# A two-block kernel on one core: the first wait of a preparation stands two pieces later, weight loads stand ahead of stores, and the last layer norm works on tokens

## What is computed

```python
def layer_norm(t, g, b):
    mu = jnp.mean(t32, axis=-1, keepdims=True)
    var = jnp.mean(jnp.square(t32 - mu), axis=-1, keepdims=True)
    y = (t32 - mu) * lax.rsqrt(var + NORM_EPS)
    return y * g + b
...
u, gate, q_mem = _split(h @ lru_w_in[j], [TOK_WIDTH, MIX_WIDTH, MEM_WIDTH])
tok = rg_lru_branch(u, ...)
y = jnp.concatenate([tok, mem_out], axis=-1) * jax.nn.silu(gate)
h = layer_norm(ALPHA * h + y @ w_out[layer], ln_g[layer], ln_b[layer])
```

## Time and profile before

| what | us |
|---|---|
| median of 3 runs | 3521.47 |
| lowest, highest | 3514.03, 3525.67 |
| the profiled execution | 3513.61 |
| its span | 3511.8 |
| PE busy in it | 3248.4 |
| DVE busy in it | 1852.3 |

### The profile page before, as it was taken

One profiled execution on the slowest core, in us unless ns is written; L12 is line 12 of the kernel. 1 busy time (PEld: TensorE's weight loads), 2 busy tenths in 40 slices (PEclk: granted clock), 3 DMA queues, 4 the chain that ended last, 5 costly groups with the idle time before them and its releaser, 6 DMA issues. The chain is left out here.

```text
span 3511.8 us, 46419 instructions
## 1 busy us (share of the span) xinstructions
PE 3248.4 (92%) x18084; PEld 2592.9 (74%) x18084; DVE 1852.3 (53%) x2662; ACT 1158.3 (33%) x2270; POOL 1555.9 (44%) x1195
## 2 busy tenths in 40 slices
PE   6898999999799999889999999999897999999796
PEld 4766787788598988668888888888775666777465
DVE  4288844546445455586633363336312666565736
ACT  5244431333333333331211021102223665145723
POOL 1215635455143341266666666665451001654432
PEclk9988879999899999999999999999997999999898
DMA  4345435232343342353333333334434221222112
GB/s 179 102 141 150 145 116 181 92 92 70 96 128 106 98 131 63 113 152 93 94 98 99 98 93 99 96 96 114 130 105 124 76 61 43 88 83 60 48 54 78
DMA packets 521310, 358.60 MB, mean 102 GB/s; under 512 B 92561, under 2 KB 477446, under 8 KB 520070
## 3 DMA queue, kind: packets, MB, share of 16 engines
q1 hardware_dynamic: 510438, 325.22, 32.0%
q0 software_dynamic: 4608, 16.78, 1.6%
q10 hardware_dynamic: 6048, 13.63, 1.1%
HBM read 276.85 MB, written 78.18 MB: 101 GB/s over the span
## 5 line engine op out<-in xcount | busy, mean ns | idle before, releaser
L2409 PE MATMUL psum<-place,place 128*128 128x512 f32 x2126 | 856.4, 403 | 63.2 <-POOL place L2387 29.3
L2410 PE MATMUL psum<-place,place 128*128 128x512 f32 x2126 | 837.8, 394 | 0.0
L2411 PE MATMUL psum<-place,place 128*128 128x512 f32 x2126 | 836.9, 394 | 0.0
L2385 POOL CAST place<-place 128x1024 fp32r<-128x1024 f32 (+3 forms) x302 | 298.3, 988 | 1097.0 <-PE psum L2411 650.1
L2387 POOL TENSOR_TENSOR place<-place,place 128x1024 fp32r<-128x1024 f32 (+3 forms) x302 | 692.1, 2292 | 24.2
L2409 PEld LDWEIGHTS psum<-place,place 128*128 128x128 f32 x2126 | 405.8, 191 | 171.5 <-issue 44.8
L2410 PEld LDWEIGHTS psum<-place,place 128*128 128x128 f32 x2126 | 405.9, 191 | 88.7 <-issue 6.6
L2411 PEld LDWEIGHTS psum<-place,place 128*128 128x128 f32 x2126 | 405.2, 191 | 87.0
L651 PE MATMUL psum<-place,place 128*128 128x512 f32 (+1 forms) x712 | 289.3, 406 | 20.9 <-issue 10.2
L652 PE MATMUL psum<-place,place 128*128 128x512 f32 (+1 forms) x712 | 274.5, 386 | 0.0
L653 PE MATMUL psum<-place,place 128*128 128x512 f32 (+1 forms) x712 | 273.9, 385 | 0.0
(11 more groups left out here) (331 smaller groups left out, 5510.7 us busy)
## 6 DMA issues: line engine op xcount, KB each, us to landing
place<-in_w_mlp_up SPq DMA_DIRECT2D x64, 512.0 KB, 4.0
place<-in_w_mlp_down SPq DMA_DIRECT2D x64, 512.0 KB, 3.9
place<-in_w_out SPq DMA_DIRECT2D x48, 512.0 KB, 4.1
chunked<-place SPq DMA_DIRECT2D x64, 320.0 KB, 3.6
place<-in_w_in SPq DMA_DIRECT2D x34, 512.0 KB, 5.6
solve<-in_w_ada POOLq DMA_DIRECT2D x32, 512.0 KB, 6.2
place<-in_lru_w_in SPq DMA_DIRECT2D x32, 512.0 KB, 3.9
place<-in_mla_w_in SPq DMA_DIRECT2D x30, 512.0 KB, 4.1
```

What stands on the lines that cost most here:

```text
L2385: nc.gpsimd.tensor_copy(hi, raw).then_inc(self.w_split, 1)
L2409: pe.matmul(ps, self.w_hi[:, j, k, :], hi, start=(k == 0), stop=False)
L2410: pe.matmul(ps, self.w_hi[:, j, k, :], lo, start=False, stop=False)
L2411: mm = pe.matmul(ps, self.w_lo[:, j, k, :], hi, start=False, stop=(k == kt - 1))
```

## The change

In `Linears.sync` the load of tile g + 1 is issued ahead of the store of tile g - 1. In `Prepare.tensor` the two waits move to the third PREP slot. `TurnOut` is replaced by `NormOut`: the second layer's norm leaves `LayerNorms`, whose units go from 4 to 2, and each block of 128 tokens is turned first (8 transposes into one of three pairs of PSUM banks); then DVE takes mean and variance of each token with `bn_stats` and `bn_aggr`, ACT takes the root of 128x1, and DVE makes the reciprocal and two passes over 128x1024. ACT issues the output's stores. The sums L2509 fall away for this layer. One block's slot (OUT) comes after each second tile of s = 1, and four more after the last tile.

```diff
@@ Linears.sync
             if c == 0 and k0 == 0 and g >= 1:
-                store(g - 1)
                 if g + 1 < G:
                     load(g + 1)
+                store(g - 1)
             yield
@@ Prepare.tensor
         yield
+        yield
         pe.wait_ge(self.fixed, 80)
         pe.wait_ge(self.astep, 1)
-        yield
@@ NormOut, in place of TurnOut
+    def tensor(self, pe):
+        C = self.C
+        for t in range(self.blocks):
+            for n in (self.first + KD * (t // 4) + KD - 2, self.first + KD * (t // 4) + KD - 1):
+                pe.wait_ge(self.chain.evac[n % 2], n // 2 + 1)
+            if t >= self.BUFS:
+                pe.wait_ge(self.centred, t - self.BUFS + 1)
...
+    def scalar(self, act):
+        def store(t):
+            act.wait_ge(self.finished, t + 1)
+            act.dma_start(rows(self.out, t), self.nat[:, t % 2]).then_inc(self.stored[t % 2], 16)
+        for t in range(self.blocks):
+            act.wait_ge(self.joined, t + 1)
+            self.C.nc.scalar.activation(self.rstd[:, t % 2], self.var[:, t % 2], ACT.Sqrt, bias=self.C.cols[:, 48:49])\
+                .then_inc(self.rooted, 1)
+            if t:
+                store(t - 1)
+            if t == self.blocks - 1:
+                store(t)
+            yield
...
+        def count(t):
+            for q in range(2):
+                dve.wait_ge(self.turned, 2 * t + q + 1)
+                nc.vector.bn_stats(self.parts[:, t % 2, 6 * q:6 * q + 6], self.turned_at(t, q)).then_inc(self.counted, 1)
+            dve.wait_ge(self.counted, 2 * t + 2)
+            nc.vector.bn_aggr(self.both[:, t % 2], self.parts[:, t % 2]).then_inc(self.joined, 1)
+        def apply(t):
+            y, r = self.nat[:, t % 2], self.rstd[:, t % 2]
+            dve.wait_ge(self.rooted, t + 1)
+            nc.vector.reciprocal(r, r).then_inc(self.inverted, 1)
+            if t == 0:
+                dve.wait_ge(self.loaded, 32)
+            if t >= 2:
+                dve.wait_ge(self.stored[t % 2], 16 * (t // 2))
+            dve.wait_ge(self.joined, t + 1)
...
+            stt(y, ps, self.mean[:, t % 2], self.g, ALU.subtract, ALU.mult).then_inc(self.centred, 1)
+            dve.wait_ge(self.inverted, t + 1)
+            dve.wait_ge(self.centred, t + 1)
+            stt(y, y, r, self.b, ALU.mult, ALU.add).then_inc(self.finished, 1)
+        half = self.blocks // 2
+        for t in range(self.blocks):
+            count(t)
+            if t % half:
+                apply(t - 1)
+            if t % half == half - 1:
+                apply(t)
+            yield
+    def sync(self, sp):
+        sp.wait_ge(self.chain.done, self.first)
+        for dst, row in ((self.g, self.gain), (self.b, self.bias)):
+            sp.dma_start(dst, row.broadcast_to([P, D])).then_inc(self.loaded, 16)
+        yield
@@ rest
+                if l == 1:
+                    tiles[-1]["nth"] = 0
...
-        for s, end in enumerate((W0 + KD, W0 + 2 * KD, W1 + KD)):
+        for s, end in enumerate((W0 + KD, W0 + 2 * KD)):
...
+        if n >= W1 + KD and (n - W1 - KD) % 2 == 1:
+            order.append(OUT)
+    order += [OUT] * (last.blocks - order.count(OUT))
```

More of the change, by code:

```diff
@@ L3534, in sync, with __init__, turned_at @@
         sp.dma_start(self.vals, self.vm.rearrange("(a p) n -> p a n", p=P)).then_inc(self.loaded[0], 16)
-class TurnOut:
-    def __init__(self, C, norm, x, out, at):
-        self.C, self.norm, self.x, self.out = C, norm, x, out
+class NormOut:
+    BUFS = 3
+    def __init__(self, C, chain, x, gain, bias, out, first, at):
+        self.C, self.chain, self.x, self.gain, self.bias, self.out, self.first = C, chain, x, gain, bias, out, first
         self.nat = C.slot(0, 2, D, at=at)
-        self.turned, self.copied = C.sem("t_turned"), C.sem("t_copied")
-        self.stored = C.pair("t_stored")
-        self.slots = T // P
+        self.g, self.b = (C.slot(0, 1, D, at=at + (2 + j) * D)[:, 0, :] for j in range(2))
+        stats = C.slot(0, 2, 24, at=at + 4 * D)
+        self.parts, self.mean, self.var, self.rstd = (stats[:, :, a:a + n] for a, n in ((0, 12), (12, 1), (13, 1), (14, 1)))
+        self.both = stats[:, :, 12:14]
+        (self.turned, self.counted, self.joined, self.rooted, self.inverted, self.centred, self.finished) = (
+            C.sem("t_" + n) for n in ("turned", "counted", "joined", "rooted", "inverted", "centred", "finished"))
+        self.loaded, self.stored = C.sem("t_loaded"), C.pair("t_stored")
+        self.blocks = T // P
+    def turned_at(self, t, q):
+        return self.C.psum[:, 2 + 2 * (t % self.BUFS) + q, :]
     def tensor(self, pe):
         C = self.C
[L3549 to L3552, removed]
+        for t in range(self.blocks):
[3 more added lines that the diff above has]
+                pe.wait_ge(self.centred, t - self.BUFS + 1)
             for q in range(2):
                 for k in range(4):
-                    mm = pe.transpose(C.psum[:, 4 + 2 * (t % 2) + q, k * P:(k + 1) * P],
-                                      self.x[:, 4 * q + k, P * t:P * t + P], C.mat("ident"))
+                    mm = pe.transpose(self.turned_at(t, q)[:, k * P:(k + 1) * P], self.x[:, 4 * q + k, P * t:P * t + P],
+                                      C.mat("ident"))
                 mm.then_inc(self.turned, 1)
@@ L3637, in rest @@
         dict(x=x_of(s), acc=small[s], rstd=small[2], sq=sq, gain=par("ln_g", 8 * l), bias=par("ln_b", 8 * l),
-             hi=half(s)[0] if l == 0 else None, lo=half(s)[1] if l == 0 else None) for l in range(2) for s in range(SEG)])
+             hi=half(s)[0], lo=half(s)[1]) for l in range(1) for s in range(SEG)])
     lru = Lru(C, chain, norm, u, gates, y_hi, y_lo, 3 * SLOT, blocks, lambda t: index["u", t, 1],
@@ L3644, in rest @@
     lru.banks_free, mem.banks_free = [(mem.copied, early), (mem.evac, early // 2 - 1)], (lru.sig, 2 * NT)
-    turned = TurnOut(C, norm, h, out, 3 * SLOT)
+    last = NormOut(C, chain, h, ins["ln_g_2"][1:2, :], ins["ln_b_2"][1:2, :], out, W1, 4 * SLOT)
     def mixed(s):
@@ L3679, in rest @@
             order += [MEM] * mem_left
-    for x in range(max(norm.slots, T // P)):
-        order += [NORM] * (x < norm.slots) + [OUT] * (x < T // P // 2)
-    order += [OUT] * (T // P // 2)
+        if n >= W1 + KD and (n - W1 - KD) % 2 == 1:
+            order.append(OUT)
+    order += [OUT] * (last.blocks - order.count(OUT))
+    head = order.index(OUT) + 1
     assert order.count(LRU) == lru.slots and order.count(MEM) == mem.slots
@@ L3692, in _ @@
             a.sync(sp)
-            alternate(only(LIN, HELD, OUT), chain.sync(sp), None, None, None, turned.sync(sp), lru.load(sp))
+            alternate([x for x in order[:head] if x in (LIN, HELD, OUT)] + [x for x in order[head:] if x in (LIN, HELD)], chain.sync(sp), None, None, None, last.sync(sp), lru.load(sp))
             for j in range(2):
-                sp.wait_ge(turned.stored[j], 16 * (T // P // 2))
+                sp.wait_ge(last.stored[j], 16 * (last.blocks // 2))
         @block.gpsimd
@@ L3706, in _ @@
             alternate(only(LIN, NORM, LRU, MEM, OUT), chain.tensor(pe), norm.tensor(pe), lru.tensor(pe), mem.tensor(pe),
-                      turned.tensor(pe))
+                      last.tensor(pe))
         @block.scalar
@@ L3714, in _ @@
             alternate(only(LIN, NORM, LRU, MEM, OUT), chain.scalar(act), norm.scalar(act), lru.scalar(act),
-                      mem.scalar(act), turned.scalar(act))
+                      mem.scalar(act), last.scalar(act))
         @block.vector
@@ L3721, in _ @@
             lru.prelude_vector(dve)
-            alternate(only(LIN, NORM, LRU, MEM), chain.vector(dve), norm.vector(dve), lru.vector(dve), mem.vector(dve))
+            alternate(only(LIN, NORM, LRU, MEM, OUT), chain.vector(dve), norm.vector(dve), lru.vector(dve),
+                      mem.vector(dve), last.vector(dve))
 def block_kernel(nc, ins, out, stop=None):
```

14 lines of the change are left out of this document (4 added, 10 removed).

## The result

The changed kernel takes 3476.15 us in the median (3468.06 to 3490.5, 4 runs) against 3521.56: a ratio of 0.9878, with a 95% interval from 0.9839 to 0.9917.

What follows compares the result with a forecast made beforehand. PE, busy 92% of the span, was taken as the bound, so gains lie where it stands still or runs slow. 4.0 + 5.0 + 13.8 = 22.8 us off the 3521.47 median gave 3498.7, range 3484 to 3514.

Steps and rivals of the forecast that it cites:

- Part A: Preparation's first wait, two slots later, and loads ahead of stores: slot 15 starts earlier, 4.0 us gained, carried to the end.
- Part B: Memory tiles, loads ahead of stores: PE's first wait of 3.52 goes, the second of 2.58 stays; 5.0 us gained.
- Part C: Last norm: 6.8 us gained inside the chain of 15 tiles and 7.0 after the last tile, 13.8 together.
- The first (A and B save nothing): Rival at the preparation and memory tiles: waits only move, the last norm alone gains; 3507.7 us, chance 0.13.
- The second (both waits close whole): Rival at the preparation and memory tiles: both bubbles vanish with their slow tiles, gain 31.4; 3490.1 us, chance 0.10.
- The third, a store behind a load: Rival in SP's queue: stores start behind 524 KB of load, costing 8.8 us at L578; 3507.5 us, chance 0.10.
- The fourth: Rival in the last norm: BN_STATS as slow as the reciprocal, 3.346 for 512 columns, 26.5 us more; 3525.2, chance 0.05.

Runs made afterwards that it cites:

- e5: Kernel before, with 6 more 128x128 matmuls ahead of the first value tile's first piece: 3509.1 us, ratio 0.9974.
- e6: Changed kernel, with 24 more 128x128 matmuls ahead of the value tile's first piece: 3495.12 us, ratio 0.9924.
- e13: Kernel before, with three 128x512 matmuls ahead of each of two narrow products between the value tile's pieces: 3508.58 us, ratio 0.9966.
- e14: Changed kernel, with three 128x512 matmuls ahead of each of two narrow products between the value tile's pieces: 3476.42 us, ratio 0.9874.
- e2: Kernel before, with only the hunk of `Linears.sync` (loads ahead of stores): 3491.49 us, ratio 0.9924.
- e7: Kernel before, with loads ahead of stores at the memory tiles alone: 3518.71 us, ratio 0.998.
- e1: Kernel before, unchanged, profiled and timed once more: 3520.23 us, ratio 1.0003.

## Why the prediction was right and wrong

**The step that failed** is the first one, what bounds the kernel, and with it a term that the sum put at nothing: the clock in the value tile and next to it, 22.0 of the 45.6 us between the two profiles. PE's stretches without idle time were taken as fixed, and only the places where it stands still were read. PE is busy there for 44.00 of 44 us, and takes about half as long for the same work in after. A granted clock of 0.50 was read where an idle time stood ahead of it, and not where none did; a row of windows over 437 to 494 would have shown it. The sum had no term and the rivals no case for it; its other terms came to 23.6 against 22.8. e5, e6, e13 and e14 show that the term isn't the load order's own: a shift of PE's work alone changes the share of executions that run the value tile at half clock. That the swap acts by such a shift, by chance to the better side, is the reading that fits e2 and e6; a part of the moved wait in it is not shown.

The median's place is in part luck. Of the four times one, 3490.5, lies on the upper level, which is inside the forecast's range. The chances took 0.3% as what a measurement of this kernel tells from no change; executions of one kernel lie 20 us, 0.6%, apart.

**Part A** was right at its place: slot 15 at 140.01 against 140.4 forecast, 3.9 gained against 4.0. That it is carried through was wrong: 4.4 are there at 208, 1.0 at 300, 2.8 at 421 and 3.9 at 437. The stretches between fall to 1.2 GHz at other moments in each execution; two profiles of before differ by 5 us at the same instruction there.

**Part B** was right: 5.9 (e7: 5.9) against 5.0, one wait gone and the other left.

**Part C** was too small: 7.5 + 9.7 = 17.2 against 6.8 + 7.0 = 13.8. In the chain PE waits nowhere now. In the tail a count measures 1.45, not 1.7, and an apply 2.60, not 2.85: 5 x 0.25 + 6 x 0.25 = 2.75, which is the 2.7 that were missing. The passes and BN_STATS were sized well, 1.27 and 1.29 against 1.3, and 2 x 0.68 against 1.37; what was too much are the gaps, since on DVE an instruction starts before the one ahead has ended (a reciprocal takes 0.11 from 3441.05, and the pass behind it starts at 3441.07).

**The rivals.** The first (A and B save nothing) falls with B's 5.9. The second (both waits close whole) falls: PE waits 5.90 and 2.83. The third, a store behind a load, is there and small: SP's waits for landed rw stores are

```profile
SPq L578 <- DMA rw<-place: 12.2, 4, 3.4
```

in after, 1.7 more than in the earlier trace rows and not 8.8, and no wait of PE for late weights is longer for it. The earlier trace rows are also only one row of L578: its waits for the gate stores, 10 of 28.1 us in all before, are 9 of 24.3 after. The Trainium skill ("DMA: Bandwidth & Descriptors", Queues, rings and completion order) has a ring's descriptors taken in order on each DMA engine; the 0.4 more per wait don't speak against it, and are far from the 2.2 that a whole load ahead of each would cost. One reason stands in the timeline of after: SP waits for ACT's emptying between the two, and of the ten rw stores from 140 to 400 us six are issued 5 to 16 us behind the load, four 0.6 to 1.2 us. Whether that is all of it was not tried. The fourth falls: BN_STATS takes 0.68, a fifth of the reciprocal's 3.346.

Without the clock's part, what is left of the change is 24 to 32: the distance between the two kernels' upper levels is some 29 (3519 and 3490), between e13 and e14 32, and the terms of the table without the value tile add up to 23.6 in the two profiles.

## What to carry to other kernels

Read the granted clock of every stretch in which the bounding engine is "busy", ahead of its waits: a stretch at 0.50 without an idle time is a term of its own, and a change that moves work ahead of it can switch it. Where times of one kernel lie at two levels, find the stretch that makes them before an edit is credited or blamed; here three wide matmuls at each of two places among the narrow ones did it, for 5.6 us. A median over a few runs of such a kernel holds the share of executions on each level as much as the edit.

## What the runs showed of the hardware

The clock fell with PE busy all the time, in matmuls of 128x128 with a few of 32 and 64 rows between them, and at 1.2 GHz a piece of 96 of 128x128 without a gap did not bring it back (450.15 to 470.89 in before; 44 us at 0.50 in all, in e1 too). It rose at 494.5, with 512 wide ones at work since 489.4. The Trainium skill ("TensorE: Matmul & The Clock Gate", Part 1: The HAM clock gate) says that the clock goes by how busy PE has been, and that this is judged in a rhythm that runs free and does not start anew with a kernel. The second agrees with the spread between executions of one kernel. The first can't be read off the busy column, which is 44.00 of 44 where the clock is low.

A matmul of two float32 operands, 128x512, took 0.92 and left two records (36 in 33.29).
